# Splitting the second halves of the recurrent mixer's q and k weights into hi and lo parts

## The reference, cut to what matters

```
def mlstm_mixer(x, w_in, b_gates, conv_w, conv_b, norm_g, w_out):
    proj = x @ w_in
    qk, v, o_pre, gates = jnp.split(proj, [2 * D, 3 * D, 4 * D], axis=-1)
    qk = jax.nn.silu(causal_conv(qk, conv_w, conv_b))
    q, k = jnp.split(qk, 2, axis=-1)
    ...
        s = jnp.einsum('bhid,bhjd->bhij', q_n, k_n) * p
```

## Time and profile before

| | |
|---|---|
| median of 3 runs | 1712.5 us (1710.53 to 1715.84) |
| the profiled execution | 1711.34 us |
| its span | 1709.5 us |
| PE busy | 1642.1 us (96%) |
| DVE busy | 1376.1 us (80%) |
| ACT busy | 1035.5 us (61%) |
| mean granted TensorE clock | 0.979 of full speed |

### The profile page before, as it was taken

The page is one execution under the profiler, slowest core; times in us unless marked ns, Lnnn a source line. Parts: engine busy times, 40 slices in busy tenths (PEclk is TensorE's granted clock), DMA queues, the critical chain, the costliest instruction groups (busy, mean ns, idle before and its releaser), DMA issues.

```text
span 1709.5 us, 23281 instructions
## 1 busy us (share of the span) xinstructions
PE 1642.1 (96%) x9114; PEld 1381.8 (81%) x9114; DVE 1376.1 (80%) x2009; ACT 1035.5 (61%) x1530; POOL 123.2 (7%) x103
## 2 busy tenths in 40 slices
PE   7999999997999999999969999999999999999998
PEld 7877878786887877878757878899988887889987
DVE  4978999999788899999999866898777965675555
ACT  6357888896334588888755554544445555454443
POOL 0001111110000111111130000000002000000000
PEclk9999999998999999999989999999998999999999
DMA  8957999894564799998655533499873432244540
GB/s 340 342 200 293 374 395 369 342 398 145 193 230 164 320 369 365 367 392 350 265 187 182 183 131 138 174 347 351 323 280 124 173 138 85 87 160 173 196 173 25
DMA packets 58790, 420.91 MB, mean 246 GB/s; under 512 B 6625, under 2 KB 6689, under 8 KB 8370
## 3 DMA queue, kind: packets, MB, share of 16 engines
q1 hardware_dynamic: 58034, 417.19, 63.5%
q0 software_dynamic: 640, 2.14, 0.4%
HBM read 418.26 MB, written 1.05 MB: 245 GB/s over the span
## 4 chain that ended last, share of the span: by engine, by line
PE 77%; DVE 15%; ACT 6%; issue 2%; DMA 0%; SPq 0%; ACTq 0%; DVEq 0%
PE ps L794 74%; DVE lo L1910 6%; ACT hi L1470 3%; DVE AR L1903 2%; PE ps L1362 1%; DVE ACC L1903 1%; PE ps L880 1%; DVE X L1903 1%; ACT AF L1658 0%; DVE AR L1900 0%; DVE AF L1903 0%; ACT AR L1634 0%; PE ps L1340 0%; DVE TINY L1903 0%; ACT AR L1811 0%
## 5 line engine op out<-in xcount | busy, mean ns | idle before, releaser
L1910 DVE TENSOR_TENSOR lo<-raw,hi 128x1024 fp32r<-128x1024 f32 x484 | 592.2, 1246 | 126.8 <-ACT hi L1470 125.3
L1470 ACT ACTIVATE hi<-raw 128x1024 fp32r<-128x1024 f32 x484 | 498.3, 1056 | 217.7 <-PE ps L794 212.2
L794 PE MATMUL ps<-hi,T 128*128 128x512 f32 x1364 | 489.0, 408 | 5.5 <-DVE T L1903 3.0
L794 PE MATMUL ps<-lo,T 128*128 128x512 f32 x916 | 360.9, 394 | 0.0
L794 PE MATMUL ps<-T,hi 128*128 128x256 f32 x1792 | 331.6, 286 | 10.2 <-DVE lo L1910 8.6
L794 PEld LDWEIGHTS ps<-hi,T 128*128 128x128 f32 x1364 | 259.1, 190 | 66.2 <-issue 12.3
L794 PEld LDWEIGHTS ps<-T,hi 128*128 128x128 f32 x1792 | 282.8, 193 | 20.8 <-DVE lo L1910 9.8
L794 PE MATMUL ps<-hi,AF 128*128 128x512 f32 x752 | 263.5, 399 | 0.4 <-DVE AF L2625 0.4
L794 PE MATMUL ps<-T,lo 128*128 128x256 f32 x896 | 254.2, 284 | 0.0
L794 PEld LDWEIGHTS ps<-lo,T 128*128 128x128 f32 x916 | 173.8, 190 | 39.8 <-issue 7.2
L794 PE MATMUL ps<-lo,AF 128*128 128x512 f32 x496 | 196.1, 395 | 0.0
(11 more groups left out here) (235 smaller groups left out, 1854.3 us busy)
## 6 DMA issues: line engine op xcount, KB each, us to landing
raw<-in_moe SPq DMA_DIRECT2D x98, 1024.0 KB, 8.0
AR<-in_moe SPq DMA_DIRECT2D x78, 1024.0 KB, 8.4
raw<-in_b_ff SPq DMA_DIRECT2D x64, 1024.0 KB, 5.0
raw<-in_ada SPq DMA_DIRECT2D x48, 1024.0 KB, 5.8
raw<-in_b_in SPq DMA_DIRECT2D x24, 1024.0 KB, 4.9
ACC<-in_moe SPq DMA_DIRECT2D x16, 1024.0 KB, 8.1
raw<-in_b_gate SPq DMA_DIRECT2D x16, 1024.0 KB, 4.8
raw<-in_ml_qk SPq DMA_DIRECT2D x8, 1024.0 KB, 5.0
```

The source lines that it names most:

```text
L794: return e.matmul(o, l, r, start=a, stop=z, skip_group_check=True)
L1470: e.activation(hi[n % NC][:, :], raw[place[c]][:, 1024 * half:1024 * half + 1024], ACT.Copy).then_inc(*to("hi", "hi", n))
L1910: tt(lo[n % NC][:, :], r, hi[n % NC][:, :], SUB).then_inc(*to("lo", "lo", n))
```

## The change

The special case for `ml_qk` goes, so that all 16 units of q and k are split.

```
 def whole(name, c):
 
-    if name == "ml_qk":
-        return 2
     return {94: 0}.get(c, (0, 0, 0, 0, 1, 0)[c % 6]) if name.startswith("moe") else 0
```

## The result

The changed kernel takes 1724.34 us (median of 6 runs, 1720.17 to 1728.36) against 1711.65 us for the kernel before on the same chip (6 runs, 1710.53 to 1715.84). The ratio is 1.0061, with a 95% interval of 1.0042 to 1.0080, so it is slower, by some 10 us (the two medians lie 12.7 us apart, the interval of the ratio spans 7 to 14 us). The forecast had the sign of its own sum right (+4.9), but the time lies above its range, whose upper end was 1721. The profiled execution took 1722.01 us with a span of 1719.9, which is 10.4 us more than before.

A forecast was written before the change was run, and what follows sets the result against it. The prediction took DVE's queue up to the silu of tile 7 to bound the q and k stretch. -0.6 + 7.96 - 2.50 = +4.9 on 1712.5 gave 1717.4, rounded to 1717.5 us, range 1713.5 to 1721.

The forecast's parts named there:

- PE gains 4.7 us: q and k stretch: eight pairs of units give PE 4.7 us less, which by itself moves nothing, PE being ahead of DVE.
- DVE pays, -0.6 + 7.96 - 2.50 = +4.9: Up to tile 7's convolution: tile 0 earlier 0.6, five splits and an ada step 7.96 more, a 2.50 wait filled.
- the 2.50 us: DVE's wait before the split at 480.71, for a rounding behind ACT's exp; forecast to go, 2.50 us.
- Where PE stands: PE's idle waits in the stretch: some 7 us before scores 2, 2 for the running maximum, about 2.7 at scores 3.
- The clock as a rival: PE's wait before scores 2 halves the clock; 2.7 of 4.5 us hidden, about 2 remain: +7, 1719.5 us; 20%.
- +4.9 passes on unchanged: From scores 3 on the chain is PE, so the 4.9 us delay reaches the end of the kernel as it is.
- clock or other late ends: Case of a half clock near scores 2 or other late ends, +6 to +9 us over before; 20%.
- The list of signs: Profile marks to check: tile convolution times, PE idle brackets, DVE chain and splits, half clock near 502 to 510.
- a silu of tile 7 as forecast and an end that is later by more: Sign that the forecast is wrong through the clock or a wait after 520 us; no size given.

The follow-up runs named there:

- h1: Kernel before, second units of q and k run as split matmuls with the first unit's hi and lo, nothing added to ACT or DVE; ratio 0.9991.
- e3: Changed kernel with the four ada steps of the q and k stretch moved out of it; ratio 1.0022 against the kernel before.
- h2: Kernel before with the subtraction for the first halves of chunks 3 to 7 of q and k done twice on DVE; ratio 1.0056.
- h3: Changed kernel with only the second halves of chunks 0 to 3 split; ratio 1.0045 against the kernel before.
- the h runs: Last four follow-up kernels: PE's part alone, DVE's part alone, first four chunks split, and that with ada steps out; ratios 0.9991, 1.0056, 1.0045, 1.0012.

## Why the prediction was right and wrong, by its steps

**PE gains 4.7 us and it moves nothing: right.** h1 has this part by itself: scores 3 move by the 0.6 us of tile 0, and PE's waits grow from 1.83 to 4.40 us.

**DVE pays, -0.6 + 7.96 - 2.50 = +4.9: right.** From tile 0's convolution to tile 7's 59.2 us were forecast (456.8 to 516) and 59.36 measured (455.83 to 515.19); that both came about 1 us early is the lead of this profile ahead of the change. Scores 3 and the start of the next stage are at +5.0. The size of a split and of an ada step, and the condition for the 2.50 us (an ada step and a split between the logits and the split that waits), held up in e3, h2 and h3.

**Where PE stands: right in place, but for one wait, and too large.** Forecast were 6 to 8 us at scores 2 (measured 5.58), about 2 at the running maximum (2.03), and 2 to 3 at scores 3 (none). The walk counted all of PE's time at full speed; the 3.4 us at half speed near 470 us and the 6.8 us behind scores 2 took the difference.

**The clock as a rival, +2 us at scores 3: the fall was right, its price was not.** The half speed came where the rival put it, 502 to 510 forecast and up to 508.8 in the trace, and it was wholly hidden: it only ate the wait at scores 3.

**"+4.9 passes on unchanged. Behind it the chain is PE, with no load in it that keeps a fixed time, so nothing gives it back": this step failed.** I asked only what could give the delay back, and put what the delay could add behind 541 us at 0. It held up to 570 us. Then the norm and router stage took 21.5 us in place of 17.65, +3.9, and later stages another +2.4. The profile of before had a sign of it, a mean clock of 0.81 in that stage, and a place that is partly at half speed can be so for longer, as here. I had looked at the clock only inside the stretch that the change touches. g1 shows the step by itself: 1.6 us of harmless matmuls in the kernel before make the same stage 3.9 us longer.

The chances followed from that. The 20% for "clock or other late ends" were priced at +6 to +9 from a half clock inside the stretch; the case "+4.9 at scores 3 and a later stage that falls into the long form" had no price. The list of signs did name it: a silu of tile 7 as forecast and an end that is later by more. Worked out with g1's step it would have given 1717.5 + 3.9 = 1721.4, outside the range, and with something for the places behind it more.

**What stays open.** Why the stage is long at some starts and short at others was not derived; the runs show only that it depends on the start and not on the change. In slices of 2 us, the clock of the kernel before falls between 568 and 570 us and is full again between 574 and 576; that of the changed kernel falls between 572 and 574 and is full again only between 590 and 592. The remaining difference isn't split by cause either: the places behind 590 us added between -0.9 and +4.8 us over the kernels, and more often added than gave back. g1, with nothing of the change in it, has the largest of these, so they don't need the change, but no run shows what sets them. The kernel before may simply have its profiled stages at favourable positions. Whether each timed run has the same stages long as the profiled one can't be seen, since only one execution of a kernel has a trace. Single executions of the kernel before also spread, in the h runs from 1707.41 us (mean clock 0.983) to 1719.33 us (0.973), so its stages need not take the profiled form each time. h3's ratio of 1.0045 is 7.7 us, where its profile, the fastest of its eight executions, has +4.6.

## What to carry to other kernels

Find by the chain and the wait brackets whose queue bounds the stretch, then count in the order what that queue passes between two landmarks; the busy share (96% PE) would have led to a forecast of the wrong sign. In these runs an idle bracket on the bounding engine was filled only by work put between the instruction that starts the chain behind it and the one that waits, not by work ahead of it. And a shift of even 1 to 5 us is not handed on as a constant: look in every later stage whose mean clock is under 1.00 for time at half speed, and let the range reach to that stage's longer form.

## What was unexpected of the hardware

The same stage, with the same instructions, takes 17.3 to 18.0 us in seven of the fourteen profiles of the table and 21.5 to 21.55 in the other seven, with nothing in between; the short form has 0.81 or 0.90 of the full clock, the long one 0.59 or 0.60. Equal idle times of 3.7 us on PE (901.30 before, 909.30 after) were followed by full speed in one kernel and half speed in the other.

A DVE instruction beside GpSimd's broadcast took far longer. DVE in the changed kernel:

```profile
524.26 3.18 DVE L1910 TENSOR_TENSOR lo<-raw,hi 128x1024 fp32r<-128x1024 f32 x1
527.36 1.21 DVE L2001 TENSOR_TENSOR X<-AR 128x1024 f32<-128x1024 f32 x1
```

and POOL in the same kernel:

```profile
523.68 2.82 POOL L2660 PARTITION_BROADCAST AR<-AR  x1 [1.94 <-DMA AR<-in_lnrow]
```

The split that takes 1.22 us elsewhere took 3.18 while the broadcast ran; the next instruction of the same size, behind it, took 1.21. In all fourteen profiles the DVE instruction of this size beside this broadcast takes 3.06 to 3.21 us. No run moves the broadcast away, so that it is the cause is argued and not shown.
